# A hybrid decoder step on one Trainium2 core: the second token group's trunk spread over eighteen expert jobs instead of fifteen, with gaps at its turns

## The chip, the core and the metric

One core of a Trainium2 chip runs the whole program. Its engines are TensorE (PE: matmuls, with its weight loads shown apart as PEld), VectorE (DVE), ScalarE (ACT), GpSimd (POOL) and SyncE (SP, which here only starts DMA transfers). The metric is the device time of one execution in microseconds (us), the median of several runs.

## What is computed

One layer of a trunk for 544 tokens (512 of a prompt, and 8 samples of 4), in float32. After a norm and one combined projection there are three branches (a diagonal state space model "S5", a convolution module, an attention into 256 memory tokens), which are gated, merged and projected. Then comes a layer of single-neuron experts: for every token 8 heads pick 16 experts each out of 16384.

```
g = sigmoid(gates)
merged = g0 * br_s5 + g1 * br_conv + g2 * br_xa
h = h + merged @ w_out
xb = rmsnorm(h);  q = xb @ w_q;  s = q . sub_keys      # 8 heads, 2 halves
experts, gate = top 16 of the pair sums of the top 16 of each half, softmax
u = u_tab[experts]                                      # a row of 1024 per token, head and place
w = gate * gelu(u . xb)
h = h + sum over 8*16 rows of w * v_tab[experts]
y = rmsnorm(h)
```

For the 8 samples the attention reads keys and values of its own from a cache in memory.

## The kernel before

The tokens stand in four tiles of 128 (t = 0 to 3) and one of 32 (t = 4). The first 256 tokens are the first group (tiles 0 and 1); the other 288 are the second group. In the first 460 us the kernel does what all tokens need together, and the trunk of the first group to its end. Then it starts the experts, and does the rest of the second group's trunk beside them.

**Expert jobs.** A job is a tile and a head; there are NJ = 34 (tile 4 packs four heads into one). A job has 16 rounds, so there are 544. Round g gathers with one indirect DMA on GpSimd (L592) 128 rows of 8 KB, the u and the v row of one expert for each token: 1.049 MB. The gathers go through a ring of ten buffers (RING); round g's gather waits until the user of round g-10 has let its buffer go. For each round, in this order:

- VectorE forms the dot product of the u half with xb (`dot`, L1876).
- Every four rounds make a group: ScalarE takes a gelu of four dots (`gelu_of`, L1274) and VectorE multiplies by the gates (`weigh`, L1891). VectorE does that for a group behind the dot of the first round of the *next* group.
- The v half is added to the accumulator in one of two ways. Mostly ScalarE builds a diagonal matrix of the weights (L1407) and TensorE multiplies it with the v row in two matmuls of 512 columns (L1058). For the last round of each group in the first SHARED jobs (`vector_rows`), VectorE adds weight times row itself (`add_row`, L1902).

So when TensorE stands at round r, VectorE is at least at the first round of the next group.

**The second group's trunk** is written as a generator on each engine (`rest_of_trunk`). TensorE takes from its own `late_matmuls(j)` steps in round j of a job: 6 where j % 4 is 3, else 2, which makes 48 in a job. A step is one matmul of 288 columns or, in a gap, nothing. The table BANK_JOBS lists the small jobs and their steps in order, and from it PLACE gives the round in which each ends. ScalarE and VectorE do their part of each in a fixed round, PLACE plus 2 to 10. The names in BANK_JOBS:

- `Aq`, `As`: the last heads' queries and key scores of the first group.
- `g{q}.{b}`, `p{q}.{b}`: gate and branch product of column block q and branch b, 8 and 4 matmuls; VectorE multiplies and adds them (L1926, L1931) in round PLACE + 8.
- `w{j}`: output projection, 8 matmuls each; it waits for all merges (`mergeb_ok`). VectorE adds it to h (L1937).
- `ssb`: sum of squares (L1010), then on VectorE its scaling (L1940, PLACE + 8), the reciprocal and the normed xb (L1943 to L1949, PLACE + 10).
- `ht`, `xt`: the turns, transposes of h and xb back into rows (L989), copied out by ScalarE (L1344, L1353).
- `q`, `s`: queries (L979, 8 matmuls each) and key scores (L1034) of the second group.

They share four PSUM banks in turn, so each small job waits until the fourth before it has been copied out. SyncE loads the weights of each (512 KB for g, w and q, 256 KB for p) as soon as the one four before has been used.

**Before the experts** TensorE's order is written by hand. `gates(0, 2)` computes two gate blocks (8 matmuls each); then come the scores of the samples' attention, `ss_s` (L730): 8 blocks of 4 matmuls, each with its own 512 KB of cached keys, through three buffers that are loaded as they come free. Then the outputs of the S5 states (`out_of_states`, L782 and L784, 72 columns) are woven with gate blocks (L810): `woven(small, large, skip)` takes one step of the large for each of the small, after the first `skip`.

## Time and profile before

| | us |
|---|---|
| median of 3 runs | 1969.55 |
| lowest and highest | 1967.14, 1969.92 |
| the profiled execution | 1968.79 |
| its span, first to last instruction | 1967.2 |

| engine | busy, share of the span |
|---|---|
| PE | 86% |
| PEld | 51% |
| DVE | 69% |
| ACT | 27% |
| POOL | 34% |

The chain of work that ended last runs 47% on PE and 36% in DMA transfers, nearly all of those gathers of expert rows. Shares of busy time are averages over two quite different phases: up to about 460 us TensorE is nearly always busy and the DMA engines about half of the time; from there to the end the DMA engines are busy nearly throughout.
### The profile page before, as it was taken

The numbers are of one execution on the slowest core, as the hardware profiler recorded it, in microseconds if no ns is written. First come the engines' busy times: TensorE is split into PE (matmuls) and PEld (weight loads), VectorE is DVE, ScalarE is ACT, GpSimd is POOL, SyncE is SP. The second block draws the span as 40 slices with busy tenths as digits, with TensorE's granted clock in tenths as the row PEclk, the third lists the DMA queues.
The fourth block names the chain that finished last, engine by engine and source line by source line (L and its number), as shares of the span: only waits on it lengthen the run. The fifth ranks groups of instructions, "written<-read, shape, count | busy, mean of one in ns | idle before, by whom it ended". The sixth has DMA issues, their size and how long they took to land.

```text
span 1967.2 us, 17805 instructions
## 1 busy us (share of the span) xinstructions
PE 1697.1 (86%) x5491; PEld 1011.1 (51%) x5491; DVE 1367.2 (69%) x3363; ACT 526.7 (27%) x1211; POOL 661.6 (34%) x605
## 2 busy tenths in 40 slices
PE   8999999999899999978989987778777767767876
PEld 7888887888555555544455543333333212323332
DVE  5998573334777777767977667777777777777755
ACT  3121143202243433312333322222222212222221
POOL 1020030001344444433443444434434444444442
PEclk9989999999999999989899999988989999998899
DMA  5452453555999999989999999999999999999996
GB/s 208 138 86 97 159 126 118 154 181 206 419 419 418 418 417 416 416 329 420 385 422 419 407 389 421 421 421 417 413 417 415 421 421 417 414 422 396 414 421 286
DMA packets 112111, 674.10 MB, mean 343 GB/s; under 512 B 12720, under 2 KB 15104, under 8 KB 42000
## 3 DMA queue, kind: packets, MB, share of 16 engines
q0 software_dynamic: 80816, 577.23, 72.2%
q1 hardware_dynamic: 30640, 94.82, 14.0%
q10 hardware_dynamic: 560, 0.92, 0.2%
q8 instruction: 44, 0.72, 0.1%
q14 instruction: 51, 0.42, 0.1%
HBM read 665.79 MB, written 6.21 MB: 342 GB/s over the span
## 4 chain that ended last, share of the span: by engine, by line
PE 47%; DMA 36%; issue 8%; DVE 4%; ACT 2%; POOL 2%; ACTq 0%; POOLq 0%; DVEq 0%; SPq 0%
DMA upper<-in_peer_uv,upper 22%; PE pair L1058 19%; DMA lower<-in_peer_uv,upper 13%; PE pair L616 7%; PE pair L627 6%; PE pair L979 5%; PE pair L929 2%; PE pair L810 1%; ACT upper L1407 1%; DVE upper L1876 1%; POOL upper L592 1%; POOL lower L592 1%; PE pair L661 1%; PE pair L671 1%; PE pair L798 1%
## 5 line engine op out<-in xcount | busy, mean ns | idle before, releaser
L1058 PE MATMUL pair<-upper 128*128 128x512 f32 (+1 forms) x1184 | 582.7, 635 | 135.8 <-ACT upper L1407 135.8
L592 POOL DMA_INDIRECT upper<-in_peer_uv,upper x324 | 372.8, 1151 | 493.4 <-PE pair L1058 429.6
L1058 PE MATMUL pair<-lower,upper 128*128 128x512 f32 (+1 forms) x792 | 383.9, 627 | 92.8 <-ACT upper L1407 92.8
L1058 PEld LDWEIGHTS pair<-upper 128*128 128x128 f32 (+1 forms) x1184 | 225.9, 197 | 430.0 <-issue 281.6
L592 POOL DMA_INDIRECT lower<-in_peer_uv,upper x220 | 249.3, 1133 | 498.7 <-PE pair L1058 316.0
L1058 PEld LDWEIGHTS pair<-lower,upper 128*128 128x128 f32 (+1 forms) x792 | 149.8, 195 | 286.9 <-issue 188.5
L1876 DVE CUSTOM_DVE_ANT_0 upper<-upper 128x1024 f32<-128x1024 f32 x172 | 210.7, 1225 | 121.5 <-DMA upper<-in_peer_uv,upper 121.5
L1876 DVE CUSTOM_DVE_ANT_0 upper<-upper,lower 128x1024 f32<-128x1024 f32 x152 | 186.0, 1224 | 97.4 <-DMA upper<-in_peer_uv,upper 97.2
L1407 ACT ACTIVATE upper<-upper 128x128 f32<-128x128 f32 (+1 forms) x494 | 164.7, 386 | 296.2 <-DVE upper L1891 296.0
L1876 DVE CUSTOM_DVE_ANT_0 lower<-lower,upper 128x1024 f32<-128x1024 f32 x116 | 142.1, 1225 | 87.8 <-DMA lower<-in_peer_uv,upper 87.7
L1274 ACT ACTIVATE upper<-upper 128x4 f32<-128x4 f32 x136 | 33.7, 248 | 627.3 <-DVE upper L1876 627.2
L979 PE MATMUL pair<-lower 128*128 128x288 f32 x704 | 185.1, 407 | 0.0
L1876 DVE CUSTOM_DVE_ANT_0 lower<-lower 128x1024 f32<-128x1024 f32 x104 | 127.2, 1223 | 71.1 <-DMA lower<-in_peer_uv,upper 71.0
L979 PEld LDWEIGHTS pair<-lower 128*128 128x128 f32 x704 | 133.7, 191 | 65.9 <-issue 37.7
L616 PE MATMUL pair<-lower 128*128 128x272 f32 x576 | 133.1, 393 | 1.5 <-ACT lower L1138 1.5
L616 PEld LDWEIGHTS pair<-lower 128*128 128x128 f32 x576 | 109.3, 190 | 24.5 <-issue 2.2
L979 PE MATMUL pair<-upper,lower 128*128 128x288 f32 x256 | 72.2, 416 | 10.7 <-DVE upper L1931 10.7
L1603 DVE SCALAR_TENSOR_TENSOR upper<-upper 128x512 f32<-128x512 f32 x120 | 80.5, 745 | 0.0
L627 PE MATMUL pair<-lower 128*128 128x256 f32 x336 | 75.4, 379 | 0.0
L979 PEld LDWEIGHTS pair<-upper,lower 128*128 128x128 f32 x256 | 49.9, 196 | 43.2 <-issue 22.5
L1274 ACT ACT_TABLE_LOAD x56 | 71.8, 1283 | 1.0
L627 PEld LDWEIGHTS pair<-lower 128*128 128x128 f32 x336 | 63.3, 190 | 8.4
(364 smaller groups left out, 1736.3 us busy)
## 6 DMA issues: line engine op xcount, KB each, us to landing
lower<-in_w_in SPq DMA_DIRECT2D x64, 512.0 KB, 7.2
lower<-in_peer_q SPq DMA_DIRECT2D x32, 512.0 KB, 8.0
lower<-in_proj SPq DMA_DIRECT2D x48, 256.0 KB, 7.0
lower<-in_w_out SPq DMA_DIRECT2D x16, 512.0 KB, 4.6
upper<-in_peer_uv,upper POOLq DMA_INDIRECT x324, 11.7
upper<-in_cache_k SPq DMA_DIRECT2D x8, 512.0 KB, 4.5
upper<-in_cache_v SPq DMA_DIRECT2D x8, 512.0 KB, 3.7
lower<-in_peer_uv,upper POOLq DMA_INDIRECT x220, 11.7
```

What stands on the lines that cost most here:

```text
L592: pool.indirect_dma_start(row(g), None, a["peer_uv"], bass.IndirectOffsetOnAxis(ap=idx[:, n % 8, j:j + 1], axis=0)).then_inc(row_in[g % RI ...
L616: mm = pe.matmul(ps[:, h, 0:HT], w[:, j, :], rhs[:, j, h * HT:(h + 1) * HT], start=(j == 0), stop=(j == k - 1))
L627: mm = pe.matmul(one_bank(ps), w[:, j, :], rhs[:, j, 0:FIRST], start=(j == 0), stop=(j == k - 1))
L661: mm = pe.matmul(ps[:, 0, 0:MEM], w[:, k, :], memT[:, k, :], start=(k == 0), stop=(k == KD - 1))
L671: mm = pe.matmul(ps[:, m, (j - 1) * P:(j + 1) * P], memT[:, k, m * P:(m + 1) * P], wring[:, s0:s0 + 2, k * P:(k + 1) * P], start=(k == 0), ...
L929: mm = pe.matmul(ps[:, 0:FIRST], w[:, k, :], xbT[:, k, :], start=(k == 0), stop=(k == KD - 1))
L979: mm = pe.matmul(ps[:, 0:REST], w[:, j, :], x[:, j, :], start=(j == 0), stop=(j == k - 1))
L1058: mm = pe.matmul(pairs[n % 2][0:rows, h, :], diag[:, (nth - 1) % DIAGS, 0:rows], row(g)[:, D + h * 512:D + (h + 1) * 512], start=(j == min ...
L1274: act.activation(gel[:, n % 2, j:j + GROUP], dots[:, n % 2, j:j + GROUP], ACT.Gelu, scale=rcol[:, t:t + 1] if t < 2 else 1.0).then_inc(gel ...
L1407: act.activation(diag[:, nth % DIAGS, 0:cols], turn, ACT.Copy, scale=weight[:, n % 8, j:j + 1]).then_inc(diag_ok, 1)
L1603: stt(v, tail, w, v, ALU.mult, ALU.add).then_inc(conv_step, 1)
L1876: dve.tensor_tensor_reduce(u, u, xb(EXPERTS[n][0]), 1.0, 0.0, ALU.mult, ALU.add, dots[:, n % 2, j:j + 1]).then_inc(u_used, 1)
```

## The change

- `late_matmuls` gives 4 instead of 6 steps in each fourth round: 40 in a job instead of 48.
- BANK_JOBS gets gaps, rounds' steps in which nothing is issued: 8 steps (`gapm`) ahead of `w0`, and 2 steps behind the `ht` transposes of each tile (`gaph`).
- VectorE's multiply and add of a branch product is due in round PLACE + 6 instead of + 8.
- SHARED is 16 instead of 12: VectorE adds its four V rows also in jobs 12 to 15, and TensorE does 16 rounds' rows less (32 matmuls of 512 columns).
- Before the experts, the second gate block moves into the samples' key products: one of its 8 matmuls follows each of the 8 cache blocks.
- The second `woven` skips 12 small steps instead of 8.

```diff
-        + GATES[0:2] + ["ss_s", "as0", "y0"] + GATES[2:4] + ["y1"] + GATES[4:6] + ["y2", GATES[6]]
+        + [GATES[0], "ss_s", GATES[1], "as0", "y0"] + GATES[2:4] + ["y1"] + GATES[4:6] + ["y2", GATES[6]]
...
-BANK_JOBS += [(f"w{_j}", KD) for _j in range(KD)] + [("gap0", 15), ("ssb", KD)]
-BANK_JOBS += [(f"ht{_t}.{_b}", 4) for _t in range(2, 5) for _b in range(2)]
+BANK_JOBS += [("gapm", 8)] + [(f"w{_j}", KD) for _j in range(KD)] + [("gap0", 15), ("ssb", KD)]
+for _t in range(2, 5):
+    BANK_JOBS += [(f"ht{_t}.{_b}", 4) for _b in range(2)] + [(f"gaph{_t}", 2)]
...
-SHARED = 12
+SHARED = 16
...
-    return 6 if j % 4 == 3 else 2
+    return 4 if j % 4 == 3 else 2
...
-            gates(0, 2)
+            gates(0, 1)
...
             ps = begin("ss_s")
             pe.wait_ge(q_masked, 1)
+            between = gate_by_gate(1, 2)
             for b in range(NB):
...
-                if b < NB - 1:
-                    mm.then_inc(c_used[b % 3], 1)
-            mm.then_inc(full[JOB["ss_s"][0]], 1)
+                    if h == HEADS - 1:
+                        mm.then_inc(c_used[b % 3] if b < NB - 1 else full[JOB["ss_s"][0]], 1)
+                next(between, None)
+            for _ in between:
+                pass
...
-            woven(out_of_states(1, 14, 28), gate_by_gate(4, 6), 8)
+            woven(out_of_states(1, 14, 28), gate_by_gate(4, 6), 12)
...
+                for _ in range(8):
+                    yield
                 pe.wait_ge(mergeb_ok, 2 * KD)
...
                 for t in range(2, 5):
                     for b in range(2):
                         yield from turned(f"ht{t}.{b}", h2T_b, t, P if t < TILES else NB * NT)
+                    for _ in range(2):
+                        yield
...
-                        yield PLACE[f"p{q}.{b}"] + 8
+                        yield PLACE[f"p{q}.{b}"] + 6
```

PLACE, the round in which a small job's last step falls (16 rounds to an expert job):

| small job | before | now |
|---|---|---|
| As7.1 | 21 | 25 |
| p7.2 | 117 | 140 |
| w0 | 119 | 147 |
| w7 | 139 | 169 |
| ssb | 147 | 179 |
| ht3.1 | 151 | 186 |
| q0.0 | 157 | 194 |
| s7.1, the last | 226 | 276 |

TensorE at the start of the output projection `w0`, before (L1058 is a round's row, L979 a trunk matmul; each L1058 pair is one round):

```order
L979 MATMUL pair<-upper,lower 128x288 [waits bank_free1,late_w_in3]
L979 MATMUL pair<-upper,lower 128x288
L1058 MATMUL pair<-upper 128x512 [waits diag_ok]
L1058 MATMUL pair<-upper 128x512
L979 MATMUL pair<-upper,lower 128x288 x2
L1058 MATMUL pair<-upper 128x512 [waits diag_ok]
L1058 MATMUL pair<-upper 128x512
L979 MATMUL pair<-upper,lower 128x288 [waits bank_free2,late_w_in0,mergeb_ok]
L979 MATMUL pair<-upper,lower 128x288 x7
```

and now (L1066 is the row, L983 the trunk matmul):

```order
L983 MATMUL pair<-upper,lower 128x288 [waits bank_free1,late_w_in3]
L983 MATMUL pair<-upper,lower 128x288
L1066 MATMUL pair<-lower,upper 128x512 [waits diag_ok]
L1066 MATMUL pair<-lower,upper 128x512
L983 MATMUL pair<-upper,lower 128x288 x2
L1066 MATMUL pair<-lower,upper 128x512 [waits diag_ok]
L1066 MATMUL pair<-lower,upper 128x512
L1066 MATMUL pair<-lower,upper 128x512 [waits diag_ok]
L1066 MATMUL pair<-lower,upper 128x512
L1066 MATMUL pair<-upper 128x512 [waits diag_ok,acc_step]
L1066 MATMUL pair<-upper 128x512
L983 MATMUL pair<-upper,lower 128x288 [waits bank_free2,late_w_in0,mergeb_ok]
```

The wait for the merges stood one round behind the last product's end (round 118), and now stands in round 144, the first of a new expert job. Three rows now stand between the last product's matmuls and the wait, where one stood.

TensorE at the turns (L989 before, L993 now, are transposes of h), before:

```order
L989 MATMUL pair<-upper 128x128 [waits bank_free1]
L1058 MATMUL pair<-lower,upper 128x512 [waits diag_ok]
L1058 MATMUL pair<-lower,upper 128x512
L989 MATMUL pair<-upper 128x128 x3
L989 MATMUL pair<-upper 128x128 [waits bank_free2]
L989 MATMUL pair<-upper 128x128 x3
L989 MATMUL pair<-upper 32x128 [waits bank_free3]
```

and now:

```order
L993 MATMUL pair<-upper 128x128 [waits bank_free1]
L993 MATMUL pair<-upper 128x128 x2
L1066 MATMUL pair<-upper 128x512 [waits diag_ok]
L1066 MATMUL pair<-upper 128x512
L993 MATMUL pair<-upper 128x128
L993 MATMUL pair<-upper 128x128 [waits bank_free2]
L1066 MATMUL pair<-upper 128x512 [waits diag_ok]
L1066 MATMUL pair<-upper 128x512
L993 MATMUL pair<-upper 128x128 x2
L1066 MATMUL pair<-upper 128x512 [waits diag_ok]
L1066 MATMUL pair<-upper 128x512
```

The turns' waits for banks 1, 2 and 3 fell within one or two rows; now each is a round or more behind the one before it.

TensorE at the samples' keys, before (L627 gates, L730 keys) and now (L628 and L731 gates, L743 keys):

```order
L627 MATMUL pair<-lower 128x256 [waits free2,w_in1]
L627 MATMUL pair<-lower 128x256 x7
L730 MATMUL pair<-upper,lower 128x256 [waits free0,free1,free3,free2,q_masked,cache_in0]
L730 MATMUL pair<-upper,lower 128x256 x3
L730 MATMUL pair<-upper,lower 128x256 [waits cache_in1]
```

```order
L743 MATMUL pair<-upper,lower 128x256 [waits free0,free1,free3,free2,q_masked,cache_in0]
L743 MATMUL pair<-upper,lower 128x256 x3
L731 MATMUL pair<-lower 128x256 [waits free3,w_in1]
L743 MATMUL pair<-upper,lower 128x256 [waits cache_in1]
L743 MATMUL pair<-upper,lower 128x256 x3
```

The eight matmuls of the second gate block left their place ahead of the keys and stand singly behind the eight cache blocks.

## Rows read from the trace of the kernel before

**Rows 1.** The page: 40 slices, DMA busy and rate; issue x, KB, median us to landing.

```profile
DMA  5452453555999999989999999999999999999996
GB/s 208 138 86 97 159 126 118 154 181 206 419 419 418 418 417 416 416 329 420 385 422 419 407 389 421 421 421 417 413 417 415 421 421 417 414 422 396 414 421 286
...
upper<-in_cache_k SPq DMA_DIRECT2D x8, 512.0 KB, 4.5
```

**Rows 2.** Stretches: us; busy (x) PE, PEld, DVE, ACT, POOL; PEclk, DMA, GB/s.

```profile
500.00:850.00 350.00, 323.82 (x1055) 196.25 (x1053) 264.33 (x640) 129.44 (x232) 154.66 (x119) 1.00 1.02 417
850.00:880.00 30.00, 20.72 (x63) 13.32 (x64) 18.40 (x45) 2.90 (x9) 8.29 (x7) 0.83 0.72 272
940.00:980.00 40.00, 35.16 (x112) 19.36 (x111) 37.25 (x88) 12.33 (x30) 19.30 (x15) 0.91 0.96 376
980.00:1110.00 130.00, 121.52 (x404) 71.46 (x404) 93.47 (x232) 39.13 (x117) 51.12 (x46) 0.96 1.02 420
1110.00:1155.00 45.00, 45.00 (x149) 26.21 (x148) 29.41 (x78) 14.45 (x44) 17.87 (x17) 1.00 0.97 370
1200.00:1900.00 700.00, 536.34 (x1105) 211.14 (x1104) 504.74 (x1328) 165.06 (x434) 300.64 (x276) 0.93 1.01 417
```

**Rows 3.** TensorE's timeline, sample keys: start us, us, line, form, records, idle before.

```profile
199.38 5.34 PE L730 MATMUL pair<-upper,lower 128*128 128x256 f32 x24
...
207.36 7.96 PE L730 MATMUL pair<-upper,lower 128*128 128x256 f32 x32 [0.44 <-DMA upper<-in_cache_k]
215.47 1.96 PE L758 MATMUL pair<-upper 128*128 128x256 f32 x8
```

**Rows 4.** Chain of waits, one gate block of 8 matmuls at the full clock.

```profile
264.15 3.45 PE pair L627 x16
```

**Rows 5.** TensorE's timeline at the last part of the states.

```profile
252.99 1.19 PE L810 MATMUL pair<-lower 128*128 128x256 f32 x2 [2.64 <-DVE upper L1686]
```

**Rows 6.** TensorE's timeline around its longest stop in the gather phase.

```profile
859.28 6.31 PE L979 MATMUL pair<-upper,lower 128*128 128x288 f32 x16 [10.73 <-DVE upper L1931]
865.43 1.88 PE L1058 MATMUL pair<-lower,upper 128*128 128x512 f32 x4
867.14 1.13 PE L979 MATMUL pair<-upper,lower 128*128 128x288 f32 x4
868.11 1.88 PE L1058 MATMUL pair<-lower,upper 128*128 128x512 f32 x4
...
872.52 4.04 PE L979 MATMUL pair<-upper,lower 128*128 128x288 f32 x16
876.40 1.88 PE L1058 MATMUL pair<-upper 128*128 128x512 f32 x4
```

**Rows 7.** VectorE's timeline there.

```profile
858.76 0.46 DVE L1931 TENSOR_TENSOR upper<-upper,lower 128x288 f32<-128x288 f32 x1
```

**Rows 8.** TensorE's timeline at the second group's turns.

```profile
953.03 0.65 PE L989 MATMUL pair<-upper 128*128 128x128 f32 x4 [1.60 <-DVE upper L1940]
956.92 0.39 PE L989 MATMUL pair<-upper 128*32 128x128 f32 x1 [3.23 <-ACT lower L1344]
```

**Rows 9.** VectorE's timeline there.

```profile
952.53 0.45 DVE L1940 TENSOR_SCALAR upper<-pair 128x288 f32<-128x288 f32 x1
...
957.29 1.95 DVE L1943 RECIPROCAL upper<-upper 128x288 f32<-128x288 f32 x1
...
964.18 1.22 DVE L1876 CUSTOM_DVE_ANT_0 upper<-upper,lower 128x1024 f32<-128x1024 f32 x1
```

**Rows 10.** GpSimd's timeline there.

```profile
961.54 0.94 POOL L592 DMA_INDIRECT lower<-in_peer_uv,upper  x1 [6.62 <-PE pair L1058]
```

**Rows 11.** Groups of instructions, 500 to 850 us: busy, mean ns, idle before, releasers.

```profile
L592 POOL DMA_INDIRECT upper<-in_peer_uv,upper x71 | 94.1, 1326 | 117.4 <-PE pair L1058 103.1 <-issue 14.3
...
L1902 DVE SCALAR_TENSOR_TENSOR upper<-upper 128x1024 f32<-128x1024 f32 x18 | 23.1, 1281 | 0.0
```

**Rows 12.** Groups of instructions, 1200 to 1900 us.

```profile
L592 POOL DMA_INDIRECT upper<-in_peer_uv,upper x164 | 179.1, 1092 | 238.5 <-PE pair L1058 207.2 <-issue 31.2
```

More of the change, by code:

```diff
@@ L802, in sample_values @@
                         yield
-            def gate_by_gate(lo, hi):
-                for n in range(lo, hi):
-                    w = loaded(GATES[n])
-                    ps = begin(GATES[n])
-                    for j in range(KD):
-                        mm = pe.matmul(one_bank(ps), w[:, j, :], nT[:, j, 0:FIRST], start=(j == 0), stop=(j == KD - 1))
-                        if j == KD - 1:
-                            mm.then_inc(full[JOB[GATES[n]][0]], 1)
-                        yield
             def woven(small, large, skip=0):
@@ L1016, in rest_of_trunk @@
                         yield from turned(f"ht{t}.{b}", h2T_b, t, P if t < TILES else NB * NT)
+                    for _ in range(2):
+                        yield
                 pe.wait_ge(xbTb_ok, KD)
```

8 lines of the change are left out of this document (added).

## The prediction, made before the changed kernel ran

> **What bounds the kernel now.** First the slices of the page [rows 1]. From slice 11 on, about 490 us, the DMA engines are busy at nine tenths and move some 420 GB/s, with four dents: slice 18 (329), 20 (385), 23 and 24 (407, 389), and 37 (396), and the last slice. Before that they are half idle and TensorE sets the pace. So from about 490 us a change gains only where it fills a dent, since the bytes stay the same, and before that only where TensorE gets through sooner.
>
> Then the dents by stretch [rows 2]. From 500 to 850 us the rate is 417, which I take as full. A dent costs its length times the missing share:
>
> - 850 to 880 us: 30 * (417 - 272) / 417 = 10.4 us.
> - 940 to 980 us: 40 * (417 - 376) / 417 = 3.9 us.
> - 1110 to 1155 us: 45 * (417 - 370) / 417 = 5.1 us.
>
> Together 19.4 us. From 1200 to 1900 us the rate is 417 again: nothing in sight there.
>
> What makes each dent is read from the timelines.
>
> **Dent one** is a wait of TensorE. It stops for 10.73 us before the first matmul of the output projection `w0`, until VectorE's L1931 [rows 6], which starts at 858.76 us [rows 7]: the last merge. By the table it is due on VectorE in round 117 + 8 = 125, and TensorE asks for it in round 118, when VectorE need only be at round 120. While TensorE stands, no ring buffer comes free, and the gathers run dry.
>
> **Dent two** is the turns. TensorE stops 1.60 us for VectorE's L1940 and 3.23 us for ScalarE's copies [rows 8], both because a bank that a turn wants is due to be copied out only rounds later (`ssb` on VectorE in round 155, asked for in about 151). GpSimd's next gather is held 6.62 us behind TensorE's row [rows 10]. In the same place VectorE works 6.9 us without a dot product, from its reciprocal at 957.29 to the next dot at 964.18 [rows 9]; a small part of the dent may be that.
>
> **Dent three** is TensorE's own load: busy 45.00 of 45 us [rows 2]. Here, in jobs 12 to 14, it does all 16 rows of a job and still the trunk.
>
> **The change in the gather phase.** TensorE's work in a group of four rounds, from starts in [rows 6]: a row takes 867.14 - 865.43 = 1.71 us, two trunk matmuls 868.11 - 867.14 = 0.97, eight of them 876.40 - 872.52 = 3.88, so 0.485 each. With three rows and 12 trunk matmuls a group takes 5.13 + 5.82 = 10.95 us; the changed one, with 10, takes 5.13 + 4.85 = 9.98. The DMA engines need for four gathers 4.19 MB, and for the weights (768 KB for each 12 matmuls of g and p) 0.79 MB before and 0.66 now: 11.9 and 11.6 us at 417 GB/s. So TensorE's reserve in a group goes from about 1.0 to 1.7 us. In itself that gives nothing, since the DMA engines set the pace there, and the total of weights is the same; it takes 276 rounds instead of 226 to bring them.
>
> Dent one: `w0` now starts in round 144, when VectorE has weighed that group and so is at round 148; the last merge is due in round 140 + 6 = 146. The wait is gone: -10.4 us. What comes next there is nothing of the trunk, since the 8 steps of `gapm` are empty and the loads of w0 to w3 wait only for products that are done. The due time of +6 could make VectorE wait for TensorE instead; but a matmul of round r is done about when VectorE is at r + 4 or r + 5, by the order of weighing. I take it at nothing, and 0.5 us a column block, 4 us, at most.
>
> Dent two: `ssb` ends in round 179, VectorE frees its bank in 187, and `ht3.1` wants it in about 185, when VectorE is past 188. The queries `q0.0` need the normed xb, due in round 189, and start in about 191, with VectorE past 192. Both waits are gone. VectorE's 6.9 us without a dot remain. I take 1.0 us as their cost, from nothing to the whole dent: -2.9 us, with -3.9 and 0 as the ends.
>
> Dent three: jobs 12 to 15 lose a row in each group. TensorE's group was 6.84 + some 12 * 0.41 (queries at 0.485, six of 22 steps are shorter key scores, which I put at half) = 11.8 us against 11.4 us of DMA; it becomes 5.13 + 4.1 = 9.2 against 11.2. (The DMA times are four gathers and 1.05 MB of weights for 22 steps, at 417 GB/s.) Gone: -5.1 us. In its place job 16 has the last query matmuls with four rows: 6.84 + 4.1 = 10.9 against 11.2 us, just covered; at most 2 us lost.
>
> VectorE pays 16 more adds of 1.281 us [rows 11], 5.1 us in a job of some 44 us. From 980 to 1110 us it was busy 72% [rows 2]; it becomes 83%, less than DMA's pace asks. They lie in VectorE's waits for rows: nothing, and what they cost without that cover is 20.5 us.
>
> A rule speaks against just this. GpSimd's instruction for a gather took 1326 ns on average from 500 to 850 us, where VectorE adds rows, and 1092 ns from 1200 to 1900 us, where it adds none [rows 11, 12]. It waited 103.1 us for TensorE in the former, so 0.23 us more for each issue is hidden. The Trainium skill, GPSIMD Engine Reference, "Specifications", says that GpSimd shares its SBUF interfaces with VectorE and contends with its instructions that have two SBUF inputs, as these adds do. The trace agrees in sign. Were each issue in the four jobs to reach the end, it would be 64 * 0.23 = 15 us; I take none.
>
> **The change before the experts.** The sample keys run from 199.38 to 215.47 us, 16.1 us for 32 matmuls [rows 3]. At the pace of a gate block, 3.45 us for 8 [rows 4], they are 13.8; the rest, 2.3 us, is waiting for cached keys. Eight gate matmuls, 3.45 us in all, are now laid between, 0.43 behind each block. With three buffers, a load has from its buffer's freeing to its use the time of two blocks, 2 * 1.73 = 3.5 us; now it has three gate matmuls more, 4.8 us. These loads take 4.5 us from issue to landing [rows 1], so nearly all of the waiting is covered. I take 2.1 of the 2.3 us as gained, with 0 as the other end. From there to the first gather TensorE is the chain, or engines that wait for TensorE, so it arrives whole.
>
> The skip of 12: the state matmuls that stand alone move, and no work goes. The stop of 2.64 us before the last part, for VectorE, is followed by matmuls at half clock, two gate records in 1.19 us [rows 5] where they take 0.43. The stop gets one gate matmul shorter. Whether the half clock comes, and for how long, may change by some 3 us either way. I take zero.
>
> **The sum**, against the profiled execution of 1968.79: -10.4 - 2.9 - 5.1 - 2.1 = -20.5 us, 1948.3. The median lies 0.76 us above the profiled execution, which gives 1949.
>
> **The rivals.**
>
> *Part of the gain only.* Dent two is VectorE's 6.9 us and stays (3.9), job 16 costs 2, the new due time 4: 1949 + 2.9 + 2 + 4 = 1958, or 1955 to 1961. For it speaks that the dent and VectorE's work lie in the same 10 us; against it that GpSimd was held from 954.9 us, before that work began.
>
> *Slower: TensorE at half clock.* More idle time may mean a lower clock. A group of 9.98 us at full clock covers 11.6 us of DMA; with a mean granted clock below 9.98 / 11.6 = 0.86 TensorE sets the pace. The 20.5 us are gone when a group takes 0.57 us more in 36 groups, 12.2 us, at a clock of 0.82; at 0.75 it takes 13.3, which is 1.7 * 36 = 61 us, and the kernel ends at 1949 + 61 = 2010. For it: the clock was 0.83 in the stretch with the long stop [rows 2]. Against it: it was 1.00 with TensorE busy 92.5% of the time (500 to 850 us) and 0.93 with 77% (1200 to 1900). Changed groups have it busy 9.98 / 11.6 = 86%, between these, so about 0.97 and 10.3 us. The Trainium skill, TensorE: Matmul & The Clock Gate, "HAM oscillation", says that waits for DMA in every pass of a loop can put TensorE back to half rate each time. That would be this rival; here gaps of 1.7 us in 11.6 decide, and the rows lie above the bound.
>
> *No change.* The ring's round trip bounds: GpSimd waits 103.1 of 350 us for TensorE to free buffers even where the DMA is full [rows 11]. If that loop and not the stops makes the dents, they only move, and the time stays at 1969 less the 2: 1967. Against it: each dent has its stop.
>
> *More.* The half clock before the experts goes (3 us), and dents smaller than my stretches go too: 1938 to 1941.
>
> **How the numbers follow.** The sum's case 0.60 (1941 to 1955), part of the gain 0.17, a remainder up to 1965 from no one cause 0.05, more 0.07, no change 0.05, slower 0.06. Forecast 1949. The range from 1941 to 1961 holds the first two and 0.03 of the remainder, which lies between 1955 and 1965: 0.80. A measurement tells about 0.2%, 4 us, from no change. Faster by more: 0.60 + 0.17 + 0.05 + 0.07 = 0.89; within: 0.05; slower: 0.06.
>
> **What would show it.** Right: no stop of TensorE above 2 us for L1939's merge or the turns; no stretch of 30 us below 400 GB/s from 490 us to the last gather; TensorE under 90% busy in jobs 12 to 14; keys and gate block together end 2 us sooner. Wrong: PEclk below 0.86 in the first nine jobs, or VectorE always behind in jobs 12 to 15, or a new dent where VectorE makes the reciprocal, in job 11.

## The result, and the profile of the changed kernel

| | before | changed |
|---|---|---|
| median of 5 runs each, same chip | 1967.14 us | 1956.24 us |
| lowest and highest | 1963.88, 1969.92 | 1954.94, 1957.88 |
| ratio to before, 95% interval | | 0.9939 [0.9926, 0.9952] |
| the profiled execution | 1968.79 | 1956.24 |
| its span | 1967.2 | 1954.6 |

The change gains 0.6%, some 11 to 12 us, of the 20.5 that were forecast. The time is inside the range of 1941 to 1961, but 7 us above the forecast of 1949 and outside the sum's case (1941 to 1955). In size it is the rival "part of the gain only" (1955 to 1961).

First the slices of the page, which answer to [rows 1] (40 slices; TensorE's clock, DMA busy and rate).

```profile
PEclk9989999999999999999989899988989999888999
DMA  5442463555999999999999999999999999999996
GB/s 209 140 87 97 161 136 116 157 173 223 420 420 418 419 418 412 419 415 386 420 417 372 420 420 419 402 423 421 421 418 417 417 408 419 409 412 422 420 421 270
```

The dents of before in slices 18 (329), 20 (385), 23 and 24 (407, 389) are gone. Two shallower ones stand now in slices 19 (386) and 22 (372), and a faint one in slice 26 (402). The windows say it by stretch, as in [rows 2] (us; busy of PE, PEld, DVE, ACT, POOL; PEclk, DMA share, GB/s), here with two stretches of the changed kernel more.

```profile
500.00:850.00 350.00, 309.25 (x975) 182.54 (x973) 269.14 (x646) 118.70 (x226) 143.14 (x122) 0.99 1.01 417
850.00:880.00 30.00, 26.77 (x83) 15.45 (x84) 22.50 (x58) 10.74 (x19) 11.36 (x10) 1.00 1.01 414
880.00:940.00 60.00, 50.30 (x146) 28.67 (x145) 47.20 (x110) 16.19 (x32) 23.06 (x21) 0.94 0.97 394
940.00:980.00 40.00, 34.54 (x110) 20.19 (x108) 30.91 (x81) 9.05 (x23) 15.29 (x14) 1.00 1.01 419
980.00:1110.00 130.00, 102.64 (x294) 53.52 (x294) 108.50 (x257) 35.84 (x85) 58.04 (x49) 0.89 0.98 401
1110.00:1155.00 45.00, 41.26 (x128) 24.51 (x128) 34.12 (x83) 11.79 (x38) 19.61 (x17) 0.92 1.01 420
...
1200.00:1300.00 100.00, 90.26 (x262) 47.40 (x262) 72.79 (x191) 32.10 (x94) 43.99 (x38) 0.95 1.00 412
```

The whole stretch of 500 to 1260 us, of before and then of the changed kernel:

```profile
500.00:1260.00 760.00, 678.87 (x2107) 390.26 (x2106) 565.73 (x1397) 239.98 (x538) 315.94 (x264) 0.97 1.00 408
```

```profile
500.00:1260.00 760.00, 658.50 (x2040) 379.60 (x2039) 589.76 (x1423) 232.44 (x517) 312.05 (x266) 0.96 1.00 413
```

Five GB/s more over 760 us are 760 * 5 / 417 = 9 us, to within 2 us by the rounding. By the prediction's own reckoning (length times the share missing to 417 GB/s) the stretches of 850 to 1300 us cost:

| stretch, us | before | changed |
|---|---|---|
| 850 to 880 | 10.4 | 0.2 |
| 880 to 940 | -0.6 (421 GB/s) | 3.3 |
| 940 to 980 | 3.9 | -0.2 |
| 980 to 1110 | -0.9 | 5.0 |
| 1110 to 1155 | 5.1 | -0.3 |
| 1155 to 1200 | -0.6 (423) | -0.3 (420) |
| 1200 to 1300 | -1.0 (421) | 1.2 |
| sum | 16.3 | 8.9 |

So 7.4 us are gained there. The starts of the dot products agree to about 1 us: job 0's first is at 487.8 us before and 482.9 now, job 17's at 1265.0 and 1251.7. That makes 4.9 us gained before the experts and 8.4 in the first seventeen jobs (777.2 us before, 768.8 now). From job 17's first dot to the end of the span it is 702.2 and 702.9 us, 0.7 us more. So the whole gather phase gives 7.7 us in these two profiles, where 18.4 had been forecast.

**Where dent one was.** TensorE's timeline of the changed kernel at the gap ahead of `w0` (start us, us, line, form, records, idle before and who ended it); L1066 is a row, L983 a trunk matmul:

```profile
900.51 3.60 PE L1066 MATMUL pair<-lower,upper 128*128 128x512 f32 x8
910.28 3.75 PE L1066 MATMUL pair<-upper 128*128 128x512 f32 x4 [6.17 <-ACT upper L1415]
913.82 2.13 PE L983 MATMUL pair<-upper,lower 128*128 128x288 f32 x4
915.74 2.17 PE L1066 MATMUL pair<-upper 128*128 128x512 f32 x4
917.75 1.13 PE L983 MATMUL pair<-upper,lower 128*128 128x288 f32 x4
918.72 1.88 PE L1066 MATMUL pair<-upper 128*128 128x512 f32 x4
```

The stop of 10.73 us for the merge [rows 6] is gone, and `w0` starts at 913.82 without a wait. But two rows run back to back in the empty steps. Behind them TensorE is ahead of the next group's weights and stops 6.17 us for ScalarE's diagonal. The row that follows takes 3.75 us where others take 1.88: half the clock. GpSimd's next gather pays for both:

```profile
914.84 1.43 POOL L593 DMA_INDIRECT upper<-in_peer_uv,upper  x1 [6.94 <-PE pair L1066]
```

**The turns.** VectorE's timeline, from the last V row added to the first weighing behind the norm; it has the same work as in [rows 9]:

```profile
1025.45 1.28 DVE L1910 SCALAR_TENSOR_TENSOR upper<-upper 128x1024 f32<-128x1024 f32 x1
1026.88 1.95 DVE L1951 RECIPROCAL upper<-upper 128x288 f32<-128x288 f32 x1
...
1033.75 1.22 DVE L1884 CUSTOM_DVE_ANT_0 lower<-lower 128x1024 f32<-128x1024 f32 x1
...
1037.19 0.15 DVE L1899 TENSOR_TENSOR upper<-upper 128x4 f32<-128x4 f32 x1
```

TensorE's timeline there:

```profile
1032.26 0.60 PE L993 MATMUL pair<-upper 128*128 128x128 f32 x4
1037.83 3.78 PE L1066 MATMUL pair<-upper 128*128 128x512 f32 x4 [4.97 <-ACT upper L1415]
```

And GpSimd's:

```profile
1042.42 2.02 POOL L593 DMA_INDIRECT upper<-in_peer_uv,upper  x1 [6.64 <-PE pair L1066]
```

The waits for banks [rows 8] are gone. VectorE works 6.87 us, from 1026.88 to 1033.75, without a dot, and then still has three dots to form before it can weigh the group at 1037.19. TensorE, with nothing of its own late, waits for that weighing, and again its next row runs at half clock (3.78 us). GpSimd is held as long as before, 6.64 us against 6.62 [rows 10].

**The keys.** TensorE's timeline, which answers to [rows 3] (L743 keys, L731 gates):

```profile
195.09 1.89 PE L743 MATMUL pair<-upper,lower 128*128 128x256 f32 x8
196.82 0.59 PE L731 MATMUL pair<-lower 128*128 128x256 f32 x2
...
210.22 1.89 PE L743 MATMUL pair<-upper,lower 128*128 128x256 f32 x8
211.94 0.59 PE L731 MATMUL pair<-lower 128*128 128x256 f32 x2
212.37 1.89 PE L773 MATMUL pair<-upper 128*128 128x256 f32 x8
```

Each pair of key block and gate matmul takes 2.16 us without idle time, 17.3 us for eight; before, it was 16.1 for the keys and 3.45 for the gate block.

### The profile page after: what moved, and what is told of

Same layout as the page of the kernel before. It is cut to its first block, busy times and chain, and to the rows that moved or that the text cites. A ratio compares the mean times of both kernels' runs of the same rounds, so it can differ in the third digit from the quotient of the medians.

```text
span 1954.6 us, 17708 instructions
## 1 busy us (share of the span) xinstructions
PE 1675.0 (86%) x5427; PEld 1001.0 (51%) x5427; DVE 1386.4 (71%) x3379; ACT 520.2 (27%) x1194; POOL 654.8 (34%) x605
## 4 chain that ended last, share of the span: by engine, by line
PE 46%; DMA 36%; issue 8%; DVE 4%; ACT 2%; POOL 2%; ACTq 0%; POOLq 0%; DVEq 0%
DMA upper<-in_peer_uv,upper 20%; PE pair L1066 19%; DMA lower<-in_peer_uv,upper 16%; PE pair L617 7%; PE pair L628 6%; PE pair L983 4%; PE pair L933 2%; PE pair L731 2%; POOL upper L593 1%; ACT upper L1415 1%; DVE upper L1884 1%; POOL lower L593 1%; PE pair L743 1%; PE pair L672 1%; PE pair L662 1%
## 5 line engine op out<-in xcount | busy, mean ns | idle before, releaser
L1066 PE MATMUL pair<-upper 128*128 128x512 f32 (+1 forms) x1144 | 573.1, 642 | 159.1 <-ACT upper L1415 159.1
L1066 PE MATMUL pair<-lower,upper 128*128 128x512 f32 (+1 forms) x768 | 375.2, 628 | 97.2 <-ACT upper L1415 97.2
L1066 PEld LDWEIGHTS pair<-upper 128*128 128x128 f32 (+1 forms) x1144 | 219.7, 199 | 439.1 <-issue 272.5
L593 POOL DMA_INDIRECT lower<-in_peer_uv,upper x220 | 243.6, 1107 | 479.6 <-PE pair L1066 291.5
L1066 PEld LDWEIGHTS pair<-lower,upper 128*128 128x128 f32 (+1 forms) x768 | 144.3, 194 | 282.3 <-issue 179.3
L1415 ACT ACTIVATE upper<-upper 128x128 f32<-128x128 f32 (+1 forms) x478 | 159.4, 386 | 305.6 <-DVE upper L1899 305.4
L983 PE MATMUL pair<-lower 128*128 128x288 f32 x704 | 193.2, 410 | 0.0
L983 PEld LDWEIGHTS pair<-lower 128*128 128x128 f32 x704 | 134.8, 192 | 79.2 <-issue 54.2
L628 PE MATMUL pair<-lower 128*128 128x256 f32 x320 | 71.9, 379 | 0.0
L983 PE MATMUL pair<-upper,lower 128*128 128x288 f32 x256 | 70.4, 410 | 0.0
L628 PEld LDWEIGHTS pair<-lower 128*128 128x128 f32 x320 | 60.3, 190 | 8.0
L983 PEld LDWEIGHTS pair<-upper,lower 128*128 128x128 f32 x256 | 49.2, 192 | 28.4 <-issue 18.7
## 6 DMA issues: line engine op xcount, KB each, us to landing
upper<-in_peer_uv,upper POOLq DMA_INDIRECT x324, 11.8
```

The costliest lines, as they stand in the source:

```text
L593: pool.indirect_dma_start(row(g), None, a["peer_uv"], bass.IndirectOffsetOnAxis(ap=idx[:, n % 8, j:j + 1], axis=0)).then_inc(row_in[g % RI ...
L628: mm = pe.matmul(one_bank(ps), w[:, j, :], rhs[:, j, 0:FIRST], start=(j == 0), stop=(j == k - 1))
L983: mm = pe.matmul(ps[:, 0:REST], w[:, j, :], x[:, j, :], start=(j == 0), stop=(j == k - 1))
L1066: mm = pe.matmul(pairs[n % 2][0:rows, h, :], diag[:, (nth - 1) % DIAGS, 0:rows], row(g)[:, D + h * 512:D + (h + 1) * 512], start=(j == min ...
L1415: act.activation(diag[:, nth % DIAGS, 0:cols], turn, ACT.Copy, scale=weight[:, n % 8, j:j + 1]).then_inc(diag_ok, 1)
```

## The experiments

Each ratio is to the kernel before, timed on the same chip, with its 95% interval. The "dents" are those of 500 to 1260 us, the missing share of 419 GB/s summed over bins of 2.5 us in the DMA view of each profile. By that view before lacks 19.7 us and the changed kernel 11.8. The share is net: bins above 419 count against the sum. The letters that the expectations give to theories are defined in them.

| kernel | edit | ratio | dents, us |
|---|---|---|---|
| changed | all parts | 0.9939 [0.9926, 0.9952] | 11.8 |
| e1_head | before, keys woven and skip 12 only | 0.9984 [0.9973, 0.9995] | 19.4 |
| e2_shared | before, SHARED 16 only | 0.9985 [0.9976, 0.9994] | 17.3 |
| e3_merge | before, gap ahead of w0 and due +6 only | 0.9987 [0.9978, 0.9996] | 15.5 |
| e12_turns | before, gaps at the turns only | 1.0008 [0.9999, 1.0017] | 19.1 |
| e8_pace4_alone | before, 40 steps in a job only | 0.9999 [0.9990, 1.0008] | 19.5 |
| e7_pace6 | changed, back at 48 steps | 0.9943 [0.9930, 0.9956] | 13.4 |
| e9_skip8 | changed, back at skip 8 | 0.9955 [0.9940, 0.9969] | 11.9 |
| e10_norm_longer | changed, VectorE's norm block longer | 1.0001 [0.9992, 1.0010] | 21.3 |
| e4_fill | changed, work in the gap ahead of w0 | 0.9949 [0.9935, 0.9962] | 12.1 |
| e5_split | changed, VectorE's norm block in four pieces | 0.9941 [0.9928, 0.9954] | 10.6 |
| e6_both | e4_fill and e5_split | 0.9933 [0.9920, 0.9946] | 9.4 |
| e11_fill_all | e6_both, and work in the other gaps | 0.9941 [0.9925, 0.9957] | 9.3 |

### The parts alone

**e1_head** takes only the part before the experts: the diff's lines on `GATES[1]`, `ss_s` and `woven`.

```diff
...
-            woven(out_of_states(1, 14, 28), gate_by_gate(4, 6), 8)
+            woven(out_of_states(1, 14, 28), gate_by_gate(4, 6), 12)
```

> The kernel before with only the two edits ahead of the experts (gate block woven into the samples' keys, second skip 12). In the profile of the changed kernel the chain from the first gate block to the first attention turn is 4.2 us shorter than before: 2.3 us from keys and gate block together, 1.9 us since the half clock behind the stop for VectorE lasted 3.4 instead of 6.8 us. Theory A: the whole 4.2 us arrives, since everything after follows TensorE: ratio to the kernel before 0.9979, 1963. Rival B: only the 2.3 us are steady and the half clock varies from run to run: 0.9988. Rival C: nothing arrives, since the gathers soak it up: 1.000.

Measured: 1963.79 against 1968.38 us, ratio 0.9984, 3.1 us by the ratio, with 1.0 and 5.3 as its ends. The dents stay as they were (19.4). From the start of the first gate block to the samples' scores it takes 20.92 us, the changed kernel 20.73, before 22.99. So the weave gives 2.1 to 2.3 us in these profiles; over all kernels the stretch takes 23.0 to 23.9 us in the old order and 20.7 to 21.1 in the new one, 2.5 us less in the mean. They arrive at the end: theory C is out. Between A (0.9979) and B (0.9988) the interval can't decide.

**e2_shared** lets VectorE add four more jobs' rows.

```diff
-SHARED = 12
+SHARED = 16
```

> The kernel before with VectorE's four V rows also in jobs 12 to 15 (SHARED 16) and nothing else. Theory A, as predicted: the dent at 1110 to 1155 us goes (5.1 us), ratio 0.9974. Rival B: VectorE's 16 adds of 1.28 us delay its dot products, or TensorE with less work falls to half clock, and the dent only moves: ratio 1.000.

Measured: ratio 0.9985, some 3 us. The window that in [rows 2] had TensorE busy 45.00 of 45 us at 370 GB/s:

```profile
1110.00:1155.00 45.00, 38.23 (x123) 21.61 (x122) 37.81 (x92) 15.51 (x46) 20.27 (x17) 0.96 1.01 409
```

TensorE has 6.8 us to spare, and the dent shrinks from 5.1 to 0.9 us by this window. VectorE's 20.5 us of adds show nowhere in the time. But of the 4.2 us by this window only 2.4 stay in the sum of the dents: from 1200 to 1300 us the rate is 416 GB/s where it was 421, and from 1152 us on TensorE now has stops of up to 5.5 us. Theory A's 0.9974 lies just outside the interval, so a part of the dent moved, as in B. Dent one stays, with a stop of 10.71 us.

**e3_merge** takes only the eight empty steps ahead of `w0` and the earlier due time.

```diff
-BANK_JOBS += [(f"w{_j}", KD) for _j in range(KD)] + [("gap0", 15), ("ssb", KD)]
+BANK_JOBS += [("gapm", 8)] + [(f"w{_j}", KD) for _j in range(KD)] + [("gap0", 15), ("ssb", KD)]
...
+                for _ in range(8):
+                    yield
...
-                        yield PLACE[f"p{q}.{b}"] + 8
+                        yield PLACE[f"p{q}.{b}"] + 6
```

> The kernel before with the 8 empty steps ahead of w0 and the merges due in round PLACE + 6, at the old pace of 48 steps in a job. Theory A, as predicted: the stop of 10.7 us goes and with it 10.4 us: ratio 0.9947. Rival B, from the profile of the changed kernel: the empty steps themselves leave TensorE idle for more than 5 us, it comes back at half clock, and a dent of some 3 us takes the place of the old one: 7.3 us, ratio 0.9963, with a PEclk of 0.50 right behind the gap.

Measured: ratio 0.9987, 2.6 us, where dent one alone was put at 10.4. That is less than either theory said (A 0.9947, B 0.9963). Two views of e3_merge say where the rest went. TensorE at the gap:

```profile
852.86 3.78 PE L1060 MATMUL pair<-lower,upper 128*128 128x512 f32 x4 [5.28 <-ACT upper L1409]
```

And the windows around the gap and around the turns:

```profile
850.00:880.00 30.00, 27.14 (x78) 16.24 (x79) 21.26 (x53) 3.59 (x11) 9.97 (x10) 0.89 0.97 381
...
940.00:980.00 40.00, 30.91 (x91) 16.22 (x90) 36.00 (x86) 13.57 (x28) 16.52 (x13) 0.87 0.88 338
```

Dent one falls to 30 * (417 - 381) / 417 = 2.6 us, with the stop and the row at half clock that theory B names; in the changed kernel it is 3.5. But the turns' dent doubles, from 3.9 to 40 * (417 - 338) / 417 = 7.6 us, which neither theory had. The gain at one place is paid back in part at the next.

**e12_turns** takes only the gaps behind the `ht` transposes.

```diff
-BANK_JOBS += [(f"ht{_t}.{_b}", 4) for _t in range(2, 5) for _b in range(2)]
+for _t in range(2, 5):
+    BANK_JOBS += [(f"ht{_t}.{_b}", 4) for _b in range(2)] + [(f"gaph{_t}", 2)]
...
+                    for _ in range(2):
+                        yield
```

> The kernel before with the 2 empty steps behind each tile's turn and nothing else: TensorE no longer asks for a bank before VectorE and ScalarE are due to free it, so its stops of 1.60 and 3.23 us go. Theory A, as predicted: the dent at the turns (3.9 us) shrinks to 1.0: ratio 0.9985. Theory O (TensorE's stops and VectorE's 6.9 us run side by side, and VectorE's alone are enough): the dent stays at 3.9 or more, ratio 1.000.

Measured: ratio 1.0008, nothing. TensorE's timeline shows the two stops for banks cut down to one of 1.86 us, and a new stop behind VectorE's block:

```profile
950.76 0.55 PE L990 MATMUL pair<-upper 128*128 128x128 f32 x3 [1.86 <-DVE upper L1943]
...
965.98 3.78 PE L1061 MATMUL pair<-upper 128*128 128x512 f32 x4 [5.98 <-ACT upper L1410]
```

The window:

```profile
940.00:980.00 40.00, 30.14 (x94) 16.23 (x93) 37.21 (x91) 12.79 (x29) 17.57 (x15) 0.91 0.93 366
```

The dent is 4.9 us by this window, where it was 3.9 with the stops for banks in place. VectorE's timelines say why, from the reciprocal to the first weighing behind it, here and then in the kernel before (whose reciprocal, at 957.29 us, is in [rows 9]):

```profile
955.02 1.95 DVE L1946 RECIPROCAL upper<-upper 128x288 f32<-128x288 f32 x1
...
965.34 0.16 DVE L1894 TENSOR_TENSOR upper<-upper 128x4 f32<-128x4 f32 x1
```

```profile
967.62 0.15 DVE L1891 TENSOR_TENSOR upper<-upper 128x4 f32<-128x4 f32 x1
```

The next group's weights come 10.32 us behind the reciprocal here, 10.33 before and 10.31 in the changed kernel (1037.19 - 1026.88), whatever TensorE did. Before, TensorE's two bank stops ended at 956.92 us, ahead of the block, and it did the rows that it was behind with while VectorE was in it. Without these stops it has done them sooner, and waits for the same weights. So the stops cost nothing of their own. That is theory O's answer (1.000), but for one point: the stops lay ahead of the block, and not beside it.

**e8_pace4_alone** only thins the trunk.

```diff
-    return 6 if j % 4 == 3 else 2
+    return 4 if j % 4 == 3 else 2
```

> The kernel before with 40 instead of 48 trunk steps in a job and nothing else: the stop for the merges stays, since the wait still comes one round behind the last product. Theory A, as predicted: thinning in itself gives nothing, 1.000, or up to 3 us where jobs 12 and 13 are less loaded. Rival B: more idle time of TensorE in each group brings more half clock, and costs 3 to 6 us, ratio 1.002 to 1.003.

Measured: ratio 0.9999. The windows:

```profile
900.00:950.00 50.00, 39.52 (x117) 23.00 (x116) 35.56 (x87) 11.85 (x25) 16.11 (x15) 0.90 0.84 337
...
1030.00:1070.00 40.00, 30.52 (x96) 16.37 (x94) 32.15 (x81) 10.44 (x26) 15.38 (x14) 0.87 0.86 343
1110.00:1155.00 45.00, 45.00 (x147) 25.98 (x146) 29.51 (x80) 13.56 (x43) 16.80 (x17) 1.00 1.02 421
```

TensorE is busy all of 45 us again, and yet the rate is 421: a lighter trunk alone also removes dent three. Its merge stop (8.76 us) makes 50 * 80 / 417 = 9.6 us, and the turns now cost 40 * 74 / 417 = 7.1. What is gained in one place is lost at the turns, and theory A's "nothing" comes out as a sum of two things that it didn't name.

### Changes to the changed kernel

**e10_norm_longer** makes each multiply of VectorE's norm block three times, nothing else. The block grows from 6.87 to 15.74 us (1028.96 to 1044.70), by 8.9 us.

```diff
+                    for i in (k - 1, k, k - 1, k):
+                        done(made)
+                        made = after(stt(xbT_b[:, i, 0:REST], h2T_b[:, i, :], c("g2", i), h2r_b, ALU.mult, ALU.mult))
```

> The changed kernel, with each of VectorE's multiplications for the normed xb made three times (16 more of some 0.47 us, and their waits: VectorE then works some 8 to 9 us longer without a dot product; the result is the same). Theory D (the dent at the turns is VectorE's): nearly all of it arrives, the dent grows by 8 us: ratio 0.9980, 1964. Theory E (TensorE's half clock at the turns): the dent grows by less than half of that: below 0.9960.

Measured: 1967.31 us, ratio 1.0001: the whole gain of the change is gone. TensorE's and GpSimd's timelines:

```profile
1048.78 3.78 PE L1066 MATMUL pair<-upper 128*128 128x512 f32 x4 [14.46 <-ACT upper L1415]
```

```profile
1053.37 2.01 POOL L593 DMA_INDIRECT upper<-in_peer_uv,upper  x1 [16.12 <-PE pair L1066]
```

The window of e10_norm_longer and behind it that of the changed kernel:

```profile
1025.00:1070.00 45.00, 29.21 (x78) 14.99 (x79) 40.31 (x98) 14.37 (x30) 16.66 (x13) 0.77 0.72 285
```

```profile
1025.00:1070.00 45.00, 37.00 (x106) 19.12 (x105) 39.61 (x96) 15.50 (x36) 19.14 (x16) 0.88 0.93 368
```

The dent grows from 45 * 49 / 417 = 5.3 to 45 * 132 / 417 = 14.2 us, by 8.9 us for 8.9 us of work. So from its present length on each further microsecond of the block costs one. If the dent of 5.3 us is the block's alone, the 6.9 us cost all of themselves but about 1.6. That last step is an inference: no run takes the block away. The time grew by 12 us, by the difference of the ratios; the 3 us beyond the dent are about what the two intervals leave open.

**e5_split** lays the eight multiplies in four rounds, two in each, and puts four empty steps ahead of the queries that need them.

```diff
-BANK_JOBS += [("q0.0", KD), ("q0.1", KD)] + [(f"xt{_t}.{_b}", 4) for _t in range(2, 5) for _b in range(2)]
+BANK_JOBS += [("gapq", 4), ("q0.0", KD), ("q0.1", KD)] + [(f"xt{_t}.{_b}", 4) for _t in range(2, 5) for _b in range(2)]
...
+                    if k % 2 == 0:
+                        yield PLACE["ssb"] + (12, 14, 15, 16)[k // 2]
```

> The changed kernel, with VectorE's normed xb taken apart: the reciprocal stays in round PLACE + 10, the four pairs of blocks come in rounds PLACE + 12, 14, 15 and 16, and 4 empty steps more stand ahead of the queries. Theory D (the dent at 1030 to 1052 us, 5.7 us, is VectorE's 6.9 us without a dot product): most of it goes, 4 of 5.7 us: ratio 0.9919, 1952.2. Theory E (it is TensorE, which has little to do at the turns, stands 5 us in a group and comes back at half clock): it stays at 5 us or grows by the 4 steps more: 0.9939 or above.

Measured: ratio 0.9941, not to be told from the changed kernel, where theory D said 0.9919. The window where the changed kernel had 368:

```profile
1025.00:1070.00 45.00, 34.83 (x90) 17.48 (x88) 43.67 (x105) 15.04 (x33) 20.24 (x16) 0.85 0.98 388
```

The dent is 3.1 us, 2.2 less where D said 4 and E none, a size that the times can't show. TensorE's stops there are 4.21, 1.93 and 4.03 us where they were 4.94 and 4.97: VectorE has the same sum of work there and is busy 43.67 of 45 us.

**e4_fill** puts eight matmuls, whose result is not used, into the empty steps ahead of `w0`.

```diff
-                for _ in range(8):
+                w = late_weights("w0")
+                ps = begin_bank("w0")
+                for j in range(8):
+                    pe.matmul(ps[:, 0:REST], w[:, j, :], nT[:, j, FIRST:], start=(j == 0), stop=(j == 7))
                     yield
```

> The changed kernel, with the 8 empty steps ahead of w0 filled by 8 matmuls of w0's weights with other data into w0's bank, which w0's own first matmul overwrites; their result is used nowhere. Theory B (empty steps leave TensorE idle for 6 us, it comes back at half clock, and its rows free the ring too late): the half clock at 910 us goes, and the dent there (3.5 us) with it: ratio to the kernel before 0.9921, 1952.7. Theory C (the dent comes from where w0 begins, its weights or its waits): it stays, 0.9939, 1956.2.

Measured: ratio 0.9949; theory B's 0.9921 lies outside the interval. TensorE's timeline at the gap (L1069 the row, L1009 the added matmuls):

```profile
905.22 3.07 PE L1009 MATMUL pair<-lower 128*128 128x288 f32 x12
910.61 1.96 PE L1069 MATMUL pair<-upper 128*128 128x512 f32 x4 [2.32 <-ACT upper L1418]
```

The stop shrinks from 6.17 to 2.32 us, the row behind it runs at full clock, and the dent there falls from 3.5 to 0.9 us. So B has the cause of this dent and not its worth. Yet the sum of the dents stays (12.1), with small ones at 975 and 1250 us in its place. Here is the first of them:

```profile
965.00:990.00 25.00, 20.66 (x59) 11.62 (x57) 19.51 (x43) 5.37 (x13) 9.55 (x9) 0.93 0.97 384
```

**e6_both** is the two together.

> Both edits, the filled steps ahead of w0 and VectorE's norm taken apart. If theories B and D hold, 3.5 + 4 us less than the changed kernel: ratio 0.9901, 1948.7, which would be the predicted time of 1949. If C and E hold: 0.9939.

Measured: 1955.23 us, ratio 0.9933, the best of all, by 1 us and within the intervals of the changed kernel. Its dents are 9.4 us. The 0.9901 of theories B and D together did not come: of their 7.5 us the dents show 2.4, and the time 1.2.

**e11_fill_all** also fills the other gaps (15 steps ahead of `ssb`, two behind each tile's turns, four ahead of the queries) with matmuls whose result is not used.

```diff
+            def idle_work(name, n):
+
+                ps = begin_bank(name)
+                for j in range(n):
+                    pe.matmul(ps[:, 0:REST], ones, merged_b[:, j % KD, :], start=True, stop=True)
+                    yield
...
```

> The kernel with both edits (filled steps ahead of w0, norm taken apart), and the other empty steps filled too: 15 ahead of ssb, 2 behind each tile's turn and 4 ahead of the queries, with matmuls of ones by the merged values, used nowhere. Theory B (TensorE's idle time and half clock hold the ring): of the 7 half clock periods between 970 and 1085 us (30.7 us in the kernel with both edits) at least half go, dents of 5.7 us there shrink to 3, ratio 0.9920. Theory I: what is left is VectorE's and the gathers' own: no change, 0.9933.

Measured: ratio 0.9941. TensorE's time at half clock between 480 and 1260 us, summed over the profile's clock records, falls from 58 to 34 us, and neither the dents (9.3 against 9.4 in e6_both) nor the time move. From 970 to 1085 us, where theory B looked, the mean granted clock rises from 0.87 to 0.94 and the rate only from 399 to 401 GB/s. So this half clock held nothing back; theory I said that.

**e7_pace6** is the changed kernel with 48 steps in a job again.

```diff
-    return 4 if j % 4 == 3 else 2
+    return 6 if j % 4 == 3 else 2
```

> The changed kernel at the old pace of 48 trunk steps in a job, everything else as changed. Theory A, as predicted: thinning in itself is worth nothing where the DMA engines set the pace, and jobs 12 to 15 have room since VectorE took a row of each group: 0.9939, the same. Theory F: the thinner trunk makes the dent at the turns larger (7.5 us in the kernel with the pace alone, 3.9 before), so the old pace is up to 3 us faster: 0.9924. Theory G: at the old pace the queries begin in an expert job where TensorE has too much to do, and 3 us are lost: 0.9954.

Measured: ratio 0.9943, the same as the changed kernel. The two kernels have their dents at other places:

```profile
850.00:880.00 30.00, 30.00 (x88) 17.77 (x89) 20.82 (x51) 5.21 (x14) 9.94 (x9) 0.90 0.95 378
...
940.00:980.00 40.00, 30.37 (x89) 15.95 (x89) 35.56 (x88) 14.44 (x31) 16.16 (x15) 0.83 0.87 333
```

That is 2.8 us, with TensorE busy throughout, and 8.1 us. The thinner trunk is worth nothing once the waits are moved and VectorE adds the rows, to within 0.2%, as theory A said.

**e9_skip8** takes back the skip.

```diff
-            woven(out_of_states(1, 14, 28), gate_by_gate(4, 6), 12)
+            woven(out_of_states(1, 14, 28), gate_by_gate(4, 6), 8)
```

> The changed kernel with the second skip back at 8. Theory A, as predicted: the skip in itself is worth nothing, and the shorter half clock ahead of the experts (3.4 instead of 6.8 us, worth 1.9 us) comes from the earlier start or varies from run to run: 0.9939. Theory H: the half clock is shorter because matmuls of 256 columns run right up to the stop: then with the skip at 8 the chain from the attention's first scores to its first turn takes 45.9 us again instead of 44.0, and the ratio is 0.9949.

Measured: ratio 0.9955 against 0.9939, which the intervals can't part. From the samples' scores to the first turn takes 45.3 us here. It took 44.0 in the changed kernel, 43.0 to 46.7 in seven others with skip 12, and 44.8 to 45.9 in five with skip 8, depending on how much of it ran at half clock. The stop itself is 2.64 us with skip 8 and 2.31 with 12:

```profile
249.50 0.67 PE L731 MATMUL pair<-lower 128*128 128x256 f32 x2 [2.31 <-DVE upper L1694]
```

## Why the prediction was right in direction and short in size

The time fell inside the range through a rival's part of it and not through the sum. Two terms of the sum were too large, by some 4 us each.

**Dent one, -10.4.** The wait went as worked out: `mergeb_ok` no longer stops TensorE, and the due time of +6 costs nothing that shows. The step that was too simple is "What comes next there is nothing of the trunk". True, but the group's own weights came next: TensorE runs through the rows of the empty steps, stops 6.17 us, and loses speed in the next row. From 850 to 940 us, 10.4 - 0.6 = 9.8 us were lost before and 0.2 + 3.3 = 3.5 are now, so the term gave 6.3 us instead of 10.4. e4_fill shows this cause by taking it away: stop, half clock and dent go together there. It doesn't show that this makes the kernel faster, since small dents came up elsewhere.

**Dent two, -2.9.** Both waits for banks went, as predicted, and the dent did not: 3.9 before, 5.0 now. This is the step that failed: "VectorE's 6.9 us without a dot remain. I take 1.0 us as their cost". The dent is about 5 us, and the block is 6.9. e10_norm_longer shows the price of more of it (8.9 us more of block, 8.9 us more of dent), and e12_turns shows why the bank stops could be taken away for nothing: the next weights came 10.3 us behind VectorE's reciprocal with and without them. The rows that spoke for this were in sight. [rows 9] and [rows 10] have VectorE's block and GpSimd's held gather in the same microseconds. I had set it aside since GpSimd was held from 954.9, before the block began at 957.29; but what TensorE lost before the block it made up during it. Four kernels in which dent one shrank or moved have a deeper dent at the turns than before (7.6 us in e3_merge, 7.1 in e8_pace4_alone, 8.1 in e7_pace6, 5.0 in the changed one); e5_split, with the block in pieces, has 3.1. That a dent close behind another one is shallower, since the ring has been refilled or the engines are out of step there, is an inference from these rows; no run isolates it.

**Dent three, -5.1.** Gone as predicted: 370 GB/s became 420, and TensorE is busy 41.26 of 45 us. e2_shared alone gives 3 us of the 5.1 in time. e8_pace4_alone shows that the thinner trunk alone removes it too, so two parts of the change pay for the same dent.

**Job 16**, "just covered; at most 2 us lost", taken at nothing. From 1200 to 1300 us TensorE is busy 90.26 of 100 us and the rate is 412, which is 1.2 us below 417, where before stood at 421, above it. So it costs 1 to 2 us, the end that I hadn't taken.

**VectorE's adds, 0.** Right. In the changed kernel VectorE is busy 83% from 980 to 1110 us, as worked out, and 76% from 1110 to 1155 with the rate at 420.

**GpSimd's longer instruction, 0.** No cost shows. The reading of 1326 against 1092 ns as contention with VectorE's adds is weakened by the changed kernel itself, with as many adds in the same stretch:

```profile
L593 POOL DMA_INDIRECT upper<-in_peer_uv,upper x72 | 83.8, 1163 | 123.7 <-PE pair L1066 109.8 <-issue 13.9
...
L1910 DVE SCALAR_TENSOR_TENSOR upper<-upper 128x1024 f32<-128x1024 f32 x18 | 23.0, 1280 | 0.0
```

The mean fell to 1163 ns with the adds unchanged, so most of the 0.23 us had another cause. Either of two parts of the change brings it down alone: the empty steps with the earlier merges (e3_merge, 1217) or the pace (e8_pace4_alone, 1167); in e1_head, e2_shared and e12_turns, which have neither, it is 1328 to 1340. Why, no run here settles. Where adds were put in alone, from 1080 to 1240 us in e2_shared, the mean of all gathers went from 1082 to 1134 ns. So what the Trainium skill says of the shared interfaces (GPSIMD Engine Reference, "Specifications") may be true here, with some 50 to 70 ns of an instruction whose length doesn't show in the time.

**Before the experts, -2.1.** The weave gave 2.26 us (22.99 - 20.73), nearly all of the 2.3 us of idle time in the keys. The first dot comes 4.9 us earlier, though. Of the rest 0.85 us stood before the first gate block, whose start lies anywhere from 190.5 to 193.3 us in kernels with the same code up to there. The other 1.9 us lie between the scores and the first turn, where the half clock lasted 3.4 us instead of 6.8. This is the term put at "some 3 us either way"; it fell on the good side in this profile and not in all. Over all profiles the first dot stands at 486.6 to 488.3 us in the five kernels with the old order and at 481.2 to 487.2 in the eight with both edits, 3.2 us earlier in the mean. So 1.7 of the 4.9 us are luck of this pair.

**The rivals.** TensorE at half clock did not come: PEclk is 0.99 from 500 to 850 us, and 0.89 from 980 to 1110, where the stops are. Behind single stops of 4.7 to 6.2 us a row ran at half clock, at 910, 992, 1024, 1037 and 1079 us, and it did not last. What the Trainium skill says under "HAM oscillation" (TensorE: Matmul & The Clock Gate), that waits for DMA in each pass of a loop keep putting TensorE back to half rate, the trace doesn't show for the short gaps here: 40.75 us idle in 350 (500 to 850 us), about 1.4 us in a group of 11.6, at a granted clock of 0.99. "No change" by the ring's round trip did not come either; but a part of it is in what e3_merge and e4_fill show, where a dent is removed and others grow. "Part of the gain only" came, with two of its three causes: VectorE's block, and job 16. Its third, the due time, cost nothing, and dent one's remainder stood in its place.

**The sum again**, by the same stretches, in us: 850 to 940 us -6.3, 940 to 1110 us 4.8 - 3.0 = +1.8, dent three -5.4, and 1155 to 1300 us 0.9 + 1.6 = +2.5. That is -7.4, and with 4.9 before the experts -12.3, against 12.55 between the two profiled executions.

**The signs.** Three of the four signs of being right came: no stop above 2 us for the merge or for a turn's bank, TensorE busy 112.83 of 130 us (87%) in jobs 12 to 14 (1036 to 1166 us), and keys and gate block 2.3 us shorter. The fourth failed, with 368 GB/s over 45 us from 1025 us on. Of the signs of being wrong, the granted clock (0.98 in the first nine jobs) and VectorE's load (79% busy in jobs 12 to 14) stayed away; the dent where VectorE makes the reciprocal, in job 11, came.

**What stays open.** The parts alone give 1.6 + 1.5 + 1.3 + 0.1 - 0.8 = 3.7 thousandths, together they give 6.1. With an interval of about one thousandth on each, this is at the edge of what could be chance; it could also be that dent one and dent two are only cheap to remove together with the load of TensorE, and no run tells. The traces give little sign of that: against the 19.7 us of before, the dents of the five parts alone shrink by 0.3 + 2.4 + 4.2 + 0.6 + 0.2 = 7.7 us, and together by 7.9, though two of the parts fill the same dent. Nor is it settled whether the skip of 12 does anything, and why small dents at 975 and 1250 us come and go between kernels that differ elsewhere.

## What to carry to other kernels

A stop that the profile names can be hidden by a block of work on another engine close behind it: taking the stop away leaves the block, which must be priced as if it were alone. Ask when the next weights come, and whether the stop moves that. A block of foreign work on the engine that feeds a ring can cost nearly its length, here probably 5 of 6.9 us and each further microsecond one. Spreading it over four rounds took 2.2 us off the dent, too little to see in the time. Empty steps in a schedule remove a wait but let their engine run ahead and stop; the next stop is then the one to be priced.

## What the runs showed of the hardware

In the gather phase a single stop of 4.9 to 6.2 us of TensorE was followed by a row at half clock (3.75 to 3.78 us for two matmuls of 512 columns instead of 1.88), each time. I had expected that of long stops and of the global mean, and not priced it at single ones: since that row lets ring buffers go, 1.9 us are added to the stop where it hurts. Where matmuls filled the gap (a stop of 2.32 us) the row took 1.96. On the other hand 24 us less at half clock in e11_fill_all bought nothing.

The mean length of one GpSimd gather instruction (those into `upper`, 500 to 850 us) varied between 1155 and 1340 ns over the kernels, with the same adds of VectorE in a job, and the time did not follow it.
